# adaLN weight parts spread over the dense stages and the turns to the experts; the filter of layer 1 built between expert items

## The reference

```python
mod = jax.nn.silu(cond) @ p['w_ada'] + p['b_ada']
sh1, sc1, g1, sh2, sc2, g2 = jnp.split(mod, 6, axis=-1)
h = rms_norm(x, p['norm1']) * (1 + sc1) + sh1
qa, ka, va, hy, qr, kr, vr, gr = jnp.split(h @ p['w_in'], split_points(), axis=-1)
...
merged = ga * (ya @ p['w_branch_a']) + gb * (yb @ p['w_branch_b']) + gc * (yc @ p['w_branch_c'])
x = x + g1 * (merged @ p['w_out'])
h2 = rms_norm(x, p['norm2']) * (1 + sc2) + sh2
x = x + g2 * moe(h2, w_router, b_router, p['moe_w1'], p['moe_w3'], p['moe_w2'])
```

## Time and profile before

| | |
|---|---|
| median of 3 runs | 1416.25 us (1415.23 to 1419.86) |
| profiled execution | 1418.04 us, its span 1416.3 us |
| busy shares of the span | PE 89%, PEld 67%, DVE 26%, ACT 15%, POOL 1% |
| read from HBM | 354.53 MB |

### The profile page before, as it was taken

How to read it: one execution, slowest core, us unless ns; L and a number is a source line. 1 busy time by engine, 2 the same in 40 slices (tenths; PEclk the granted TensorE clock), 3 DMA queues, 4 the chain that set the end, 5 groups by cost and what they waited for, 6 DMA issues and landing times.

```text
span 1416.3 us, 18385 instructions
## 1 busy us (share of the span) xinstructions
PE 1261.4 (89%) x7732; PEld 955.8 (67%) x7732; DVE 372.7 (26%) x922; ACT 216.4 (15%) x428; POOL 12.0 (1%) x27
## 2 busy tenths in 40 slices
PE   2679999999987999999866999999999699999992
PEld 1358888878876666666433888887888576666651
DVE  1222223332335111111042321533142621111103
ACT  2021011322011100011021210123200201000001
POOL 1000000000000000000000000000000000000000
PEclk9789999999996999999978999999999699999997
DMA  9964433424441999999989343333344089999980
GB/s 392 419 268 149 148 128 125 140 106 148 150 171 53 423 420 421 420 421 420 420 329 406 130 149 119 134 127 119 124 149 156 19 354 420 420 421 420 421 335 31
DMA packets 49788, 358.47 MB, mean 253 GB/s; under 512 B 5632, under 2 KB 5648, under 8 KB 6816
## 3 DMA queue, kind: packets, MB, share of 16 engines
q1 hardware_dynamic: 47808, 348.15, 61.8%
q0 software_dynamic: 1888, 9.03, 1.6%
HBM read 354.53 MB, written 2.62 MB: 252 GB/s over the span
## 4 chain that ended last, share of the span: by engine, by line
PE 82%; DMA 7%; DVE 6%; ACT 2%; issue 2%; SPq 0%; DVEq 0%; POOL 0%; ACTq 0%
PE bank L586 26%; PE bank L813 14%; PE bank L849 8%; PE bank L727 6%; PE bank L796 5%; DMA ring<-in_weights 4%; PE bank L742 4%; PE bank L890 3%; PE bank L512 3%; DMA ring<-in_experts 3%; PE bank L578 3%; PE bank L566 1%; PE bank L828 1%; ACT gates L1275 1%; DVE h L1354 1%
## 5 line engine op out<-in xcount | busy, mean ns | idle before, releaser
L586 PE MATMUL bank<-h,ring 128*128 128x256 f32 x1664 | 373.7, 385 | 13.8 <-ACT h L1064 13.8
L586 PEld LDWEIGHTS bank<-h,ring 128*128 128x128 f32 x1664 | 318.5, 193 | 62.8 <-issue 18.3
L813 PE MATMUL bank<-ring,gates 128*64 128x256 f32 x2048 | 225.6, 380 | 5.3 <-ACT gates L1275 3.7
L813 PEld LDWEIGHTS bank<-ring,gates 128*64 128x64 f32 x2048 | 151.1, 137 | 77.4 <-issue 7.7
L849 PE MATMUL bank<-ring,gates 128*64 128x512 f32 x512 | 113.4, 594 | 5.4 <-ACTq L1278 5.4
L512 PE MATMUL bank<-ring,condT 128*32 128x256 f32 x768 | 60.5, 483 | 45.4 <-DMA ring<-in_weights 37.0
L849 PEld LDWEIGHTS bank<-ring,gates 128*64 128x64 f32 x512 | 41.5, 137 | 66.9 <-issue 66.9
L512 PEld LDWEIGHTS bank<-ring,condT 128*32 128x32 f32 x768 | 33.3, 138 | 69.7 <-issue 62.7
L796 PE MATMUL bank<-uc,gates 128*128 128x128 f32 x576 | 72.1, 287 | 0.0
L796 PEld LDWEIGHTS bank<-uc,gates 128*128 128x128 f32 x576 | 70.8, 204 | 0.0
L1362 DVE SCALAR_TENSOR_TENSOR gates<-gates,bank 128x512 f32<-128x512 f32 (+1 forms) x18 | 11.8, 658 | 204.0 <-issue 148.6
(11 more groups left out here) (232 smaller groups left out, 1019.7 us busy)
## 6 DMA issues: line engine op xcount, KB each, us to landing
ring<-in_experts SPq DMA_DIRECT2D x204, 1024.0 KB, 10.9
ring<-in_weights SPq DMA_DIRECT2D x128, 1024.0 KB, 5.6
par<-in_params POOLq DMA_DIRECT2D x2, 781.5 KB, 10.6
cst<-in_consts POOLq DMA_DIRECT2D x1, 1537.0 KB, 11.7
x<-in_x_in POOLq DMA_DIRECT2D x1, 1024.0 KB, 20.1
sc<-in_s_cache POOLq DMA_DIRECT2D x2, 512.0 KB, 16.4
y_out<-h POOLq DMA_DIRECT2D x1, 1024.0 KB, 4.2
kc<-in_k_cache POOLq DMA_DIRECT2D x2, 256.0 KB, 13.3
```

The lines of the kernel that those rows point to most:

```text
L586: last = pe.matmul(bank[b][:, c * TOK:(c + 1) * TOK], w[:, k, c * P:(c + 1) * P], h[:, k, :], start=(k == 0), stop=(k == KT - 1))
L813: last = pe.matmul(bank[b][64 * j:64 * j + 64, half * 256:half * 256 + 256], hgat[:, k, 64 * j:64 * j + 64], w[j][:, k, :], start=(k == 0) ...
```

## The change

The order of the pieces is now a list, `weight_plan`, which SP follows and from which the waits of the other engines are counted. Of the adaLN parts only 0 and 1 of layer 0 stand ahead of the projections. Parts 2, 3 and 4 of each layer stand behind units 1, 3 and 5, their transposes one unit later; part 5 between `norm_sum` and `route`. Part 1 of layer 1 goes into the merge of layer 0, part 0 of layer 1 in front of `ranks` of layer 0. Filter steps 0 to 3 of layer 1 follow expert items 4 to 7 of layer 0, step 4 follows the jump at the end of that layer. The table of retention decays (small operations of ScalarE and VectorE) moves behind unit 2. ScalarE now copies all four blocks of turned tokens, of which VectorE had copied two. The small zero matmul behind each part is gone. POOL loads x before the constants and the caches of layer 0 only when part 1 is done. VectorE reads the block count and jumps before it waits for the last combination. At the end scale and norm are one operation in place of two, and y goes out in two halves. Biases and norm gains have a load of their own (`modp`), and `modT` exists for both layers.

```diff
+def weight_plan():
+    plan = []
+    for layer in range(DEPTH):
+        if layer == 0:
+            plan += [("ada", 0, 0), ("ada", 0, 1)]
+        for u in range(U_MERGE):
+            plan.append(("proj", layer, u))
+            if u in (1, 3, 5):
+                plan.append(("ada", layer, 2 + u // 2))
+        for m in range(6):
+            plan.append(("merge", layer, m))
+            if m == 2 and layer + 1 < DEPTH:
+                plan.append(("ada", layer + 1, 1))
+        plan += [("out", layer, u) for u in range(U_OUT, N_PROJ)]
+        plan.append(("ada", layer, 5))
+        if layer + 1 < DEPTH:
+            plan.append(("ada", layer + 1, 0))
+        plan.append(("moe", layer, 0))
+    return plan
...
-            pool.dma_start(cst[:, :], consts).then_inc(s_consts_in, 16)
             pool.dma_start(shd[:, :], shared).then_inc(s_shared_in, 16)
             pool.memset(condT[:, :, :], 0.0).then_inc(s_cond_zero, 1)
             pool.memset(ones[:, :], 1.0).then_inc(s_ones_set, 1)
-            pool.memset(zeros[:, :], 0.0).then_inc(s_zeros_set, 1)
+            pool.dma_start(x[:, :, :], x_in).then_inc(s_x_in, 16)
+            pool.dma_start(cst[:, :], consts).then_inc(s_consts_in, 16)
+            pool.dma_start(modp[:, :, :], mod_params).then_inc(s_mod_params_in, 16)
             for layer in range(DEPTH):
                 if layer:
                     pool.wait_ge(s_params_used, layer - 1 + 1)
                 pool.dma_start(par[:, :], params[layer, :, :]).then_inc(s_params_in, 16)
                 if layer == 0:
-                    pool.dma_start(x[:, :, :], x_in).then_inc(s_x_in, 16)
+                    pool.wait_ge(s_mod_ready, ada_at(0, 1) + 1)
...
-            pool.dma_start(y_out, h[:, :, :]).then_inc(s_stored, 16)
-            pool.wait_ge(s_stored, 16 * (4 * DEPTH + 1))
+            for half in range(2):
+                pool.wait_ge(s_y_ready, half + 1)
+                pool.dma_start(y_out[:, 4 * half:4 * half + 4, :],
+                               h[:, 4 * half:4 * half + 4, :]).then_inc(s_stored, 16)
+            pool.wait_ge(s_stored, 16 * (4 * DEPTH + 2))
...
-                pe.matmul(bank[q % 2][0:32, 510:512], zeros[:, 0:32], zeros[:, 0:2], start=True,
-                          stop=True, skip_group_check=True).then_inc(s_mod_rows, 1)
-            def ada_turn(layer, q):
-                pe.wait_ge(s_mod_rows_copied, 6 * layer + q + 1)
-                take(2 + q % 2)
+            def ada_turn(layer, q, b):
+                n = ada_at(layer, q)
+                pe.wait_ge(s_mod_rows_copied, n + 1)
+                take(b)
                 for t in range(2):
-                    last = pe.transpose(bank[2 + q % 2][:, t * P:(t + 1) * P],
-                                        uc[:, 8 + q % 4, t * P:(t + 1) * P], ident)
+                    last = pe.transpose(bank[b][:, t * P:(t + 1) * P],
+                                        mod_row[:, n % 2, t * P:(t + 1) * P], ident)
...
+                        if layer + 1 < DEPTH and (half, branch) == (0, 0):
+                            ada(layer + 1, 1, 4)
+                        if layer + 1 < DEPTH and (half, branch) == (1, 1):
+                            ada_turn(layer + 1, 1, 4)
...
+                norm_sum(2 * layer)
+                if layer == 0:
+                    filter_step(0, 0)
+                    pe.wait_ge(s_cond_ready, 1)
+                    ada(0, 0, 0)
+                    filter_step(0, 1)
+                    ada_turn(0, 0, 2)
+                    filter_step(0, 2)
+                    ada(0, 1, 1)
+                    ada_turn(0, 1, 3)
+                    filter_step(0, 3)
                 for u in range(U_MERGE):
                     proj(layer, u)
+                    if layer == 0 and u == 1:
+                        filter_step(0, 4)
+                    if u in (1, 3, 5):
+                        ada(layer, 2 + u // 2, 4)
+                    if u in (2, 4, 6):
+                        ada_turn(layer, 1 + u // 2, 4)
...
                 norm_sum(2 * layer + 1)
+                ada(layer, 5, 0)
                 route(layer)
+                ada_turn(layer, 5, 1)
                 tokens_turn(layer)
+                if layer + 1 < DEPTH:
+                    ada(layer + 1, 0, 2)
                 ranks(layer)
+                if layer + 1 < DEPTH:
+                    ada_turn(layer + 1, 0, 0)
...
+                    if layer + 1 < DEPTH and p >= 4:
+                        filter_step(layer + 1, p - 4)
...
+                if layer + 1 < DEPTH:
+                    filter_step(layer + 1, 4)
             norm_sum(2 * DEPTH)
...
+            def mod_rows(layer, q, b):
+                n = ada_at(layer, q)
+                sc_e.wait_ge(s_weights_used, END["ada", layer, q])
+                if n >= 2:
+                    sc_e.wait_ge(s_mod_sum, n - 1)
+                sc_e.activation(mod_row[:, n % 2, :], bank[b][:, 0:256], ACT.Copy).then_inc(
+                    s_mod_rows_copied, 1)
+                sc_e.wait_ge(s_mod_rows_copied, n + 1)
+                sc_e.sem_inc(s_bank_free[b], 1)
...
+                for n in range(4):
                     sc_e.wait_ge(s_tokens_turned, 4 * layer + n + 1)
-                    b = (4, 6, 7, 4)[n]
-                    sc_e.activation(htok[:, n // 2, 512:1024], bank[b][:, :], ACT.Copy).then_inc(
-                        s_tokens_copied_s, 1)
-                    sc_e.wait_ge(s_tokens_copied_s, 2 * layer + (n + 1) // 2)
+                    b = (4, 6, 7, 3)[n]
+                    sc_e.activation(htok[:, n // 2, 512 * (n % 2):512 * (n % 2) + 512], bank[b][:, :],
+                                    ACT.Copy).then_inc(s_tokens_copied, 1)
...
+                norm_mean(2 * layer)
+                if layer == 0:
+                    dve.wait_ge(s_consts_in, 16)
+                    dve.wait_ge(s_params_in, 16)
+                    sine_arg(0, 0)
+                    norm_inverse(0)
+                    sine_arg(0, 1)
+                    mod_add(0, 0, 2)
+                    taps_decay(0)
+                    mod_add(0, 1, 3)
+                else:
+                    norm_inverse(2 * layer)
+                norm_scale(layer, 0)
+                if layer == 0:
+                    taps_scale(0)
...
-                for n in (0, 2):
-                    dve.wait_ge(s_tokens_turned, 4 * layer + n + 1)
-                    b = (4, 6, 7, 4)[n]
-                    link(dve.tensor_copy(htok[:, n // 2, 0:512], bank[b][:, :]))
-                    dve.sem_inc(s_bank_free[b], 1)
-                    dve.sem_inc(s_tokens_copied, 1)
...
+                        mod_add(layer, 5, 1)
+                        if layer + 1 < DEPTH:
+                            mod_add(layer + 1, 0, 0)
...
-                dve.wait_ge(s_combined, ITEMS * (layer + 1))
...
+                    dve.wait_ge(s_combined, ITEMS * (layer + 1))
                     for i in range(MORE):
...
+                dve.wait_ge(s_combined, ITEMS * (layer + 1))
                 for b in range(4):
...
-            norm(2 * DEPTH, None)
-            dve.sem_inc(s_y_ready, 1)
+            norm_mean(2 * DEPTH)
+            norm_inverse(2 * DEPTH)
+            for k in range(KT):
+                link(stt(h[:, k, :], x[:, k, :], H("final")[:, k:k + 1], rmsi[:, :], ALU.mult, ALU.mult))
+                if k % 4 == 3:
+                    dve.sem_inc(s_y_ready, 1)
```

More of the change, by code:

```diff
@@ L547, in filter_step @@
                     pe.wait_ge(s_taps_abs, layer + 1)
-                    take(6)
+                    take(4)
                     for c in range(2):
-                        last = pe.matmul(bank[6][:, :], ones[:, :], habs[:, c, :], start=(c == 0),
+                        last = pe.matmul(bank[4][:, :], ones[:, :], habs[:, c, :], start=(c == 0),
                                          stop=(c == 1))
@@ L1135, in unit @@
+                norm_shift(layer, 0)
                 def unit(u):
@@ new lines, in taps_decay, with taps_scale @@
+            def taps_decay(layer):
+                for c in range(2):
+                    dve.wait_ge(s_taps_sum, 2 * layer + c + 1)
+                    link(tt(hs[:, c, :], bank[4 + c][:, :], C("decay"), ALU.mult))
+                    dve.sem_inc(s_bank_free[4 + c], 1)
+                dve.sem_inc(s_taps_decayed, 1)
+            def taps_scale(layer):
+                dve.wait_ge(s_taps_norm, layer + 1)
+                link(dve.reciprocal(tmp[:, :], bank[4][:, :]))
+                dve.sem_inc(s_bank_free[4], 1)
+                link(tt(hs[:, :, :], hs[:, :, :], tmp[:, :].unsqueeze(1).broadcast_to([P, 2, C_B]),
+                        ALU.mult))
+                dve.sem_inc(s_taps, 1)
@@ L1418, in _ @@
[L1418 to L1425 removed]
+                modT = mod_all[:, layer, :, :]
@@ L1641, in _ @@
                             u += 1
+                        if layer + 1 < DEPTH and (half, n) == (1, 0):
+                            mod_add(layer + 1, 1, 4)
                 for u in range(U_OUT, N_PROJ):
```

(2 more changed lines are left out.)

340 lines of the change are left out of this document (178 added, 162 removed).

## The result

| | before | after |
|---|---|---|
| median | 1418.05 us (4 runs, 1415.23 to 1421.13) | 1331.24 us (4 runs, 1329.55 to 1335.81) |
| profiled execution | 1418.04 us | 1331.29 us, its span 1329.5 us |
| PE, PEld, DVE, ACT, POOL busy | 89, 67, 26, 15, 1% | 94, 71, 28, 17, 1% |

The ratio is 0.9396, with a 95% interval of 0.9379 to 0.9413: 86.8 us less, 6% faster. The prediction had 1336 (1320 to 1356).

The account below looks back on a forecast made before the run. The adaLN stages were taken as bound by loading 24 MB per layer beside an idle TensorE, projections and experts as bound by TensorE. The terms -52 + 30 + 5 - 2 + 4 - 56 - 4 - 7 = -82 gave 1336 us (1320 to 1356).

Parts of the forecast that it names:

- 1 start: Before layer 0's first projection: only two parts and filter steps 0 to 3 remain, first projection near 45 us; -52 us.
- 2 projections of layer 0: Three parts at 4.3 us each stand unhidden between the matmuls, plus filter step 4 at +5 us; no wait for pieces.
- 2 merge of layer 0: One part placed in layer 0's merge, costing 4.3 us because nothing hides it.
- 2 dense part of layer 1: Three parts among layer 1's projections, 4.3 us each, with no wait for pieces.
- 3 turn to the experts, layer 0: Part 5 fills the wait before route, route perhaps 2 us sooner, part 0 of layer 1 before ranks; -2 us.
- 3 the same, layer 1: Turn to layer 1's experts: part 5 fills the wait before route and ranks can go at once; -4 us.
- 4 experts of layer 0: Filter steps 0 to 3 of layer 1 among the expert items cost TensorE time only; +4 us.
- 5 turn between the layers: From layer 0's experts to layer 1's first projection: jump, filter step 4, norm sum, wait for h; 21.0 us, -56.
- 6 end: End of program: early jump saves 2.73 us, single operations for h 3.4, y in halves perhaps 1; -7 us.
- Rival a: Dense stages: pieces come mildly late, 2 to 5 us for each of seven parts, 1350 to 1371; 0.16 together with rival b.
- rival b: Dense stages: parts run at 1.2 GHz or turn over badly, +17 us, 1353; chance 0.16 together with Rival a.
- rival d: Spread parts: each finds no piece loaded and waits 10.6 us, 106 for ten, 1442, slower than before; chance 0.02.

Follow-up runs that it names:

- E6: Changed kernel with another order at the start: part 0 ahead of filter step 0, part 1 ahead of step 2, step 3 behind the first unit; 1332.26 us.
- E4: Changed kernel with parts 2, 3 and 4 of both layers in a row behind unit 3, instead of behind units 1, 3 and 5; 1354.58 us.
- E3: Changed kernel with filter steps 0 to 3 of layer 1 moved back behind the jump, in front of step 4; 1351.69 us.
- E5: Changed kernel with the third and later ring pieces of layer 1 held back until TensorE has jumped and stands in filter step 4; 1326.75 us.
- E10: E1 with eight more 1 MB loads into unused ring slots, keeping the DMA engines busy during the jump at the end; 1340.15 us, one run.
- E1: Changed kernel with VectorE's jump back in its old place, behind the wait for the last combination; 1335.91 us.

## Why the prediction was right

The predicted sum was -82, the measured difference of the profiled executions -86.8. By its terms, from the earlier trace rows and the windows of after:

| step | predicted | measured |
|---|---|---|
| 1 start | -52 | -53.8 |
| 2 projections of layer 0 (three parts, spectrum) | +18.1 | +16.2 |
| 2 merge of layer 0 (one part) | +4.3 | +4.2 |
| 2 dense part of layer 1 (three parts) | +12.9 | +13.0 |
| 3 turn to the experts, layer 0 | -2 | -2.4 |
| 3 the same, layer 1 | -4 | -2.5 |
| 4 experts of layer 0 | +4 | +3.1 |
| 5 turn between the layers | -56 | -56.7 |
| experts of layer 1 | 0 | -0.2 |
| 6 end | -7 | -7.7 |

A single term is known to 1 or 2 us only. In the repeat of the same kernel the projections of layer 0 take 261.0 us (262.3 here), the turns to the experts 34.7 and 36.9 (36.1 and 35.8), the turn between the layers 21.1 (20.4) and the dense part of layer 1 326.9 (328.3). What the table bears out are the large terms; agreement to a few tenths is chance.

**Start.** The time is where it was put: `par` landed at 23.95 us (24 predicted), part 1 ended at 39.6 (near 42), and the first projection stands at 43.13 (near 45). The two parts took 5.08 and 5.32 us instead of 6.0 and 6.1, which is most of the 1.9 us. E6 shows that more was not to be had from the order alone.

**Parts in the dense stages.** The parts ran at full clock, 3.66 us each, and none waited for a piece. A part with all that hangs on it was put at 4.3 us; it came to 4.2 and 4.3 in the merge and in layer 1, and to 3.7 in layer 0's projections (16.2 less 5.2 for the spectrum, by three). E4 shows that the missing wait is no matter of course: with no units between the parts the full wait appears. The spare of 3 us, in which the prediction took all four pieces as loaded after the part before, was mis-sized to the safe side: it is 5 to 7 us (E4). Rival a has its price at zero in this kernel, rival b too (granted clock 0.99), and rival d is real in the form of E4. The last full-size matmul of the spectrum and the first of a part in four column strips meet in the same 0.1 us, and that part takes 3.66 us like the one in the earlier trace rows:

```profile
62.79 1.02 PE L598 MATMUL bank<-va,cst 128*128 128x512 f32 x2
63.74 3.66 PE L553 MATMUL bank<-ring,condT 128*32 128x256 f32 x64
```

The drain in the rule weighed in the prediction (the Trainium skill, TensorEngine Tiling (Array Packing), Key Properties: a change of tiling mode drains TensorE) leaves no pause that the trace shows: behind that part the next unit begins at 67.33, within 0.1 us of the part's end, and takes 7.17 us for 32 records where others take 7.07. Whatever a change costs lies inside the 4.3 us that a part came to at most, on the average of a stage, 0.7 above their own 3.66 with transposes and all.

**Turns to the experts.** This is the term where a reason was wrong. I had `route` 2 us faster once TensorE worked in front of it. From its first matmul to its end it was 9.0 us (420.94 to 421.65 and 8.29) and is 8.9 now (387.59 to 389.67 and 6.86):

```profile
387.59 0.37 PE L798 MATMUL bank<-shd,h 128*128 128x16 f32 x2 [0.46 <-ACT h L1126]
...
389.67 6.86 PE L798 MATMUL bank<-shd,h 128*128 128x16 f32 x26 [0.35 <-ACT h L1126]
...
403.63 0.62 PE L810 MATMUL bank<-rt,cst 128*128 128x16 f32 x4
...
1043.61 1.04 PE L810 MATMUL bank<-rt,cst 128*128 128x16 f32 x4 [3.11 <-DVE rt L1436]
```

Part 5 does fill the wait, 0.46 us being left of it, and `route` then goes at the pace of h, with a wait of some 0.35 us before each pair of matmuls for its first part, and ends as late after it. What was gained stands behind `route`: from its end to `ranks` it is 7.1 us against 8.7 in the earlier trace rows. In layer 1, where the prediction let `ranks` go at once, it waits 3.11 us for VectorE. In layer 0, part 0 of layer 1 fills the place of that wait and costs next to nothing (36.1 us for the turn against 35.8 in layer 1). The chain of some thirty operations of VectorE, most of 0.16 to 0.20 us, is the bound there, and the removed copies were worth only what they added to it. That is the 1.5 us by which the term for layer 1 was too large (2.6 by the repeat). That the term for layer 0 came out at -2.4 where -2 was forecast is luck in part: `route` gave nothing, 1.6 us came between `route` and `ranks` and 0.7 behind them.

**Filter among the experts.** +3.1 against +4, and 2.8 when E3 takes the steps away. Step 4 and the parts' pieces did not disturb the experts: in layer 0 TensorE waited for no piece.

**Turn between the layers.** Jump 5.61 (5.64 predicted), step 4 7.1 us (5.2 and 1.5 at the lower clock), first matmul 4.05 after the norm sum (3.99); together 20.4 against 21.0. The prediction let the jump begin at 703.75, where VectorE's began, 0.95 us behind the last combination (702.80); TensorE's begins at once. The prediction had two lengths of a jump from the rows, 5.64 us with busy DMA engines and 2.73 with idle ones, and took the longer. That the traffic is the cause was only argued there; E5 and E10 show it. The page of the Trainium skill that was cited, Runtime: NRT & Kernel Launch, Instruction fetch mechanics, says that a taken branch out of the window makes the engine fetch the target by DMA; these runs agree and add the number, 2.5 to 3.0 us with the DMA engines quiet and 5.3 to 5.6 with them full. The fetch itself is in the traces: around the jump of E5 (671 to 676 us) the two DMA queues named "instruction" bring 3 packets, 0.04 MB, and no other queue brings anything; around that of the changed kernel (669 to 677 us) they bring 4 packets, 0.05 MB, beside 2.88 MB of ring pieces.

**End.** -7.7 against -7. Of this, by the trace of E1, 3.7 us are VectorE's early jump, 1 more than the 2.73 that the prediction counted, because the reading of the block count in front of it went too; 2.9 are the single operations for h (4.24 us for eight, against 7.1 before), and the 1.1 left is what the two halves of y give.

## What to carry to other kernels

Work that depends on nothing recent belongs under matmuls that leave the DMA engines idle, in portions that the ring can refill in between: here four pieces behind two units, while three portions in a row brought back 20 us of waits in two layers. A chain of short steps over several engines goes between items of a stage whose results are wanted much later; in the open it costs its waits and the lower clock that follows from them. Before a jump over code, look at what the DMA queues are doing: holding back loads that are not yet needed took 2.7 us off the jump and 1.9 us off the work behind it.

## What was not expected of the hardware

That the traffic makes half of a jump was a guess from two rows and is now shown from both sides: TensorE 5.61 us with ring loads running and 2.87 without; VectorE 2.96 us at the quiet end and 5.45 with eight loads beside it. The granted clock decides between two speeds of the same matmuls, 2.4 and 1.2 GHz: two matmul records of step 4 took 2.05 us after a pause of 5.61 us (granted clock 0.50) and 1.10 after one of 2.87 (1.00), both behind a busy stretch. The length of the last pause alone does not tell it: in E3, with only two short steps since the jump, step 2 ran at 0.50 after a pause of 2.29 us. At the start it falls out differently from run to run (step 2 of the filter 1.98 or 3.78 us), and in the two profiled runs with the long form the first projection began 2.9 us later. What decides it there stays open.
